# Layer ends of a float32 hybrid network: first tiles of the input before the weights, and all weight remainders on VectorE

## What is computed

```python
for layer in range(2):                      # attention, then the gated recurrence
    h = rmsnorm(x, pre_norm_w[layer])
    y = mixer(h, ...)                       # (o * silu(z)) @ w_out (+ b_out)
    x = x + rmsnorm(y, post_norm_w[layer])
h = rmsnorm(x, norm_w)                      # third layer: GLA and a delta rule side by side
merged = concat([gla_out, rwkv_out])
x = x + merged @ w_out
return rmsnorm(x, final_norm_w)
```

## Time and profile before

| | us |
|---|---|
| median of 3 runs | 3806.75 (3806.06 to 3808.11) |
| the profiled execution, its own time | 3811.12 |
| its span, from first to last instruction | 3809.8 |
| PE busy | 3559.3 (93%) |
| PEld busy | 2743.4 (72%) |
| DVE busy | 1993.4 (52%) |
| ACT busy | 1653.6 (43%) |
| POOL busy | 1196.5 (31%) |

### The profile page before, as it was taken

One profiled execution on the slowest core, in us unless ns is written; L12 is line 12 of the kernel. 1 busy time (PEld: TensorE's weight loads), 2 busy tenths in 40 slices (PEclk: granted clock), 3 DMA queues, 4 the chain that ended last, 5 costly groups with the idle time before them and its releaser, 6 DMA issues.

```text
span 3809.8 us, 80205 instructions
## 1 busy us (share of the span) xinstructions
PE 3559.3 (93%) x33632; PEld 2743.4 (72%) x33632; DVE 1993.4 (52%) x4558; ACT 1653.6 (43%) x3040; POOL 1196.5 (31%) x1470
## 2 busy tenths in 40 slices
PE   7899989999799999999997979999999997999799
PEld 4555557778678887878785867777777775788677
DVE  4655554255555556555553445656667665343322
ACT  2444443132455556555553334443444442444422
POOL 0000001132444445454544323222222220444432
PEclk9999999999899999999997989999999998999999
DMA  3000000132211010111111332111111113222322
GB/s 123 34 1 1 1 12 17 34 118 87 68 28 41 23 45 23 40 29 38 30 34 72 133 126 56 41 41 41 41 41 41 40 36 107 77 73 67 100 78 89
DMA packets 220230, 202.76 MB, mean 53 GB/s; under 512 B 7072, under 2 KB 191840, under 8 KB 219872
## 3 DMA queue, kind: packets, MB, share of 16 engines
q1 hardware_dynamic: 219872, 197.62, 16.8%
HBM read 164.04 MB, written 33.55 MB: 52 GB/s over the span
## 4 chain that ended last, share of the span: by engine, by line
PE 77%; DVE 9%; ACT 7%; POOL 3%; issue 3%; DMA 1%; SPq 0%; POOLq 0%; ACTq 0%; DVEq 0%
PE bank L194 18%; PE bank L196 16%; PE bank L195 16%; PE bank L452 5%; ACT arena L188 3%; PE bank L2386 2%; DVE arena L690 2%; PE bank L1236 2%; PE bank L2397 2%; ACT L282 1%; ACT arena L189 1%; PE bank L492 1%; PE bank L316 1%; PE bank L2400 1%; PE bank L2455 1%
## 5 line engine op out<-in xcount | busy, mean ns | idle before, releaser
L195 PE MATMUL bank<-hT_cut,arena_cut 128*128 128x512 f32 x2080 | 820.2, 394 | 0.0
L188 ACT ACTIVATE arena<-bank 128x512 f32<-128x512 f32 (+1 forms) x584 | 314.8, 569 | 559.4 <-PE bank L196 332.0
L194 PE MATMUL bank<-hT_cut,arena_cut 128*128 128x512 f32 x1112 | 501.2, 451 | 9.2 <-DVE arena L183 9.2
L188 ACT ACTIVATE arena<-arena 128x512 f32<-128x512 f32 (+3 forms) x690 | 353.6, 550 | 263.1 <-POOL arena L1426 192.0
L195 PEld LDWEIGHTS bank<-hT_cut,arena_cut 128*128 128x128 f32 x2080 | 394.9, 190 | 82.2 <-issue 18.5
L196 PE MATMUL bank<-hT_cut,arena_cut 128*128 128x512 f32 x1112 | 439.0, 395 | 0.0
L189 ACT ACTIVATE arena<-arena 128x256 f32<-128x256 f32 (+2 forms) x336 | 210.3, 627 | 503.2 <-DVE arena L178 276.9
L194 PE MATMUL bank<-arena_cut,hT_cut 128*128 128x512 f32 (+1 forms) x960 | 366.8, 382 | 56.4 <-POOL oT_cut L999 51.4
L195 PE MATMUL bank<-arena_cut,hT_cut 128*128 128x512 f32 (+1 forms) x960 | 360.0, 375 | 0.0
L2662 POOL TENSOR_TENSOR arena_cut<-arena,arena_cut 128x256 fp32r<-128x256 f32 x272 | 219.2, 836 | 433.0 <-ACT arena_cut L188 433.0
L194 PE MATMUL bank<-oT_cut,arena_cut 128*128 128x512 f32 x712 | 311.1, 437 | 29.9 <-DVE hT_cut L2708 16.4
(11 more groups left out here) (238 smaller groups left out, 7067.3 us busy)
## 6 DMA issues: line engine op xcount, KB each, us to landing
arena<-in_w_in SPq DMA_DIRECT2D x100, 512.0 KB, 3.9
arena<-in_rec_w_in SPq DMA_DIRECT2D x64, 512.0 KB, 4.1
x_after<-arena SPq DMA_DIRECT2D x32, 512.0 KB, 2.6
arena<-x_after SPq DMA_DIRECT2D x32, 512.0 KB, 4.1
oT<-in_x SPq DMA_DIRECT2D x16, 512.0 KB, 3.5
arena<-in_x SPq DMA_DIRECT2D x16, 512.0 KB, 3.5
h_after<-hT SPq DMA_DIRECT2D x4, 2048.0 KB, 7.7
hT<-h_after SPq DMA_DIRECT2D x4, 2048.0 KB, 16.8
```

The source lines that it names most:

```text
L188: return e.activation(out, a, f, bias=bias, scale=scale)
L194: pe.matmul(out, a[0], b[0], start=start, stop=False)
L195: pe.matmul(out, a[0], b[1], start=False, stop=False)
```

## The change

At all three layer ends:

- ScalarE first waits for the steps in the new list `k.ready` (one of TensorE and one of VectorE, named by each phase: what the memory of tiles 0 and 1 of oT and hT waits for), then does `cut(0)`, two early pieces, `cut(1)`, the other early pieces, and only then `settle` and the later pieces.
- GpSimd starts with the remainders of tiles 0 and 1, then `settle`. It subtracts no weights.
- VectorE subtracts all eight pieces, the early ones ahead of its `settle`, each in one instruction of 1024 columns.
- TensorE waits for one semaphore, `w_v`, piece by piece in the same order as before.

```diff
@@ attention_gate @@
     k.freed = [(0, z_pe.by("z", (KC - 1) * NG - 1))]
+    k.ready = [z_pe.by("z", (KC - 1) * NG), z_v.by("o", (KC - 1) * NG)]
...
@@ finish_layer @@
-    freed = dict(k.freed)
+    freed, ready = dict(k.freed), k.ready
...
-    w_a, w_v, w_p = k.steps("wo_rounded", "hi"), k.steps("wo_rest", "lo"), k.steps("wo_first_rest", "lo")
+    w_a, w_v = k.steps("wo_rounded", "hi"), k.steps("wo_rest", "lo")
...
-                    pe.wait_ge(*(w_p.by("lo", early.index(c)) if c in freed else w_v.by("lo", later.index(c))))
+                    pe.wait_ge(*w_v.by("lo", order.index(c)))
...
-        for c in early:
+        for done in ready:
+            a.wait_ge(*done)
+        cut(0)
+        for c in early[:2]:
+            rounded(c)
+        cut(1)
+        for c in early[2:]:
             rounded(c)
         k.settle(a)
-        cut(0)
-        cut(1)
         for c in later:
             rounded(c)
...
-        for n, c in enumerate(early):
-            pool.wait_ge(*w_a.by("hi", n))
-            for i in range(4):
-                part_of = slice(256 * i, 256 * i + 256)
-                ins = pool.tensor_tensor(wo_lo[:, c, part_of], wo[:, c, part_of], wo_hi[:, c, part_of], ALU.subtract)
-            ins.then_inc(*w_p.did("lo"))
-        k.settle(pool)
         cut(0)
         cut(1)
+        k.settle(pool)
...
-        k.settle(v)
-        for n, c in enumerate(later):
-            v.wait_ge(*w_a.by("hi", len(early) + n))
+        for n, c in enumerate(early + later):
+            if n == len(early):
+                k.settle(v)
+            v.wait_ge(*w_a.by("hi", n))
             v.tensor_tensor(wo_lo[:, c, :], wo[:, c, :], wo_hi[:, c, :], ALU.subtract).then_inc(*w_v.did("lo"))
...
@@ recurrence @@
+    k.ready = [Fpe.by("v", UN - 2), Bv.by("out", UN // 2 - 1)]
@@ gla @@
+    k.ready = [Fpe.by("z1", UN - 1), Bv.by("out1", 1)]
```

More of the change, by code:

```diff
@@ L204, in __init__ @@
         self.every, self.stores, self.known = [], [], {}
-        self.before, self.freed = [], []
+        self.before, self.freed, self.ready = [], [], []
         self.bank = [ctx.enter_context(nc.psum_tensor(f"bank{i}", [P, 512], F32))[:, :] for i in range(8)]
```

## The result

The changed kernel takes 3781.52 us in the median (3779.83 to 3782.65, 4 runs) against 3806.40 for the kernel before in the same comparison. The ratio is 0.9929, with a 95% interval of 0.9918 to 0.9941. It is faster by 24.9 us, clear of what a measurement can miss. Two repeats on later occasions gave 3779.25 against 3807.79 (ratio 0.9924, 0.9912 to 0.9936) and 3778.87 against 3806.23 (0.9926, 0.9913 to 0.9938), so the three differences are 24.9, 28.5 and 27.4 us. The profiled execution took 3782.65 us with a span of 3781.2, 28.6 less than the span before.

What follows compares the result with a forecast made beforehand. TensorE was taken as the bound, waiting 51.4 us for tile 0 on GpSimd at three layer ends. Gains of 0.8 + 11.2 + 11.9 = 23.9 us from 3806.75 gave a median of 3783 us, range 3773 to 3792.

Steps and rivals of the forecast that it cites:

- What bounds it: TensorE, 77% of the chain; its waits for tile 0's remainder on GpSimd, 51.4 us at three layer ends, are the target.
- 48th matmul: Last matmul of tile 0 at each layer end; its start measures the end, forecast gains 0.8, 11.2 and 11.9 us.
- The line of subtractions: At the long layer ends, eight VectorE pieces and four GpSimd tiles take turns: 19.1 us at most, taken as 18.8.
- The first end: First layer end: one early piece, transfers hold piece 2, TensorE runs through from 764.3; gain 0.8 us, sign uncertain.
- the rise at the old moment: First layer end: TensorE's clock rises when it did before, putting tile 0's last matmul at 775.2 instead of 776.0.
- The sum: Gains at the three layer ends, 0.8 + 11.2 + 11.9 = 23.9 us, under half of the 51.4 us of waits.
- rival 1: VectorE and GpSimd subtractions exclude each other less; tile 0's start sets its end: gain 34.5 us, 3772 us; chance 0.08.
- Rivals 2 and 3: TensorE's clock low through tile 0: 3798.5 us, chance 0.08; low on into tile 1: 3817 us, chance 0.04.
- Rival 4: Gain eaten later, or ScalarE reaches tile 0 later than the code order says: 3805 us; chance 0.06.
- The signs to look for: TensorE's waits ahead of tile 0 shrink from 51.4 to some 20 us, ended by L1063; restarts near 760.7, 2041.6, 3605.

Runs made afterwards that it cites:

- the two runs with tiles moved: Changed kernel, with GpSimd waiting for VectorE's eighth piece before tile 2 in one run, before tile 1 in the other: 3775.00 and 3774.16 us.
- the run with the order alone: Changed kernel's ScalarE order, but GpSimd still subtracts the early pieces as in the kernel before: 3797.08 us against 3805.47, ratio 0.9979.
- the kernel with tiles 1 to 3 later: Changed kernel, with GpSimd waiting for VectorE's eighth piece before tile 1: 3774.16 us; repeated, 3774.51 against 3778.87 for the changed kernel.

## Why the forecast was right, point by point

- **What bounds it, and that a gain at a layer end is kept.** Right: 176.3 us behind the last 48th matmul in both kernels.
- **The line of subtractions.** Forecast: 8 x 1.21 + 4 x 2.36 = 19.1 at most, taken as 18.8 us. Measured: 18.3 us at the second end. The 48th matmul was forecast at 58.1 - 37.5 = 20.6 us and, at the third end, 21.6 - 0.7 = 20.9 us after VectorE's last write began; it came at 19.9 and 20.2. Gains of 11.9 and 12.6 us instead of 11.2 and 11.9.
- **The first end.** The step that was mis-sized. Its own working gives 776.47 - 776.0 = 0.5 us or, with the rise at the old moment, 1.3, and 0.8 was put between them. Piece 2 was forecast 7.5 us after VectorE's last write and came at 7.35, but the forecast added 11 more matmuls at 0.43 from there. The clock rose at the second of them, and the gain was 2.5 us. In the thirteen profiles of this study the number of low pitches at this end was between 0 and 12 with no order that I can name, so that this term erred on the gainful side was luck.
- **The sum.** 27.0 us in the layer ends against a forecast of 23.9; the median moved by 24.9, and by 28.5 and 27.4 in the repeats. The range said to reach down to rival 1 stopped at 3773, 1 us above it.
- **Rival 1, no exclusion (3772 us).** Refuted by the durations, and by the two runs with tiles moved. The rule of the Trainium skill, page "SBUF — State Buffer", section "Who interferes with whom", agrees with the trace: 2.36 + 1.21 = 3.57 against 3.41 measured.
- **Rivals 2 and 3, the clock stays low.** They did not occur in the changed kernel, where the clock rose after 5 to 7 low pitches and stood at 1.00 in spite of the pause of 1.68 us (columns as in the earlier trace rows):

```profile
2035.00:2045.00 10.00, 5.90 (x15) 4.27 (x16) 9.59 (x6) 9.46 (x10) 5.71 (x2) 0.55 0.86 305
2045.00:2055.00 10.00, 8.32 (x36) 6.32 (x36) 8.23 (x5) 1.75 (x4) 6.80 (x2) 1.00 0.16 65
```

The mechanism is real, though, and the run with the order alone met a part of it, with pauses of 1.7 to 3.1 us: 14 and 18 low pitches, not the whole tile, and at its third end a fall from 1.00 back to 0.50. The Trainium skill (page "TensorE: Matmul & The Clock Gate", section "HAM oscillation — how this bites in real kernels") tells of a kernel that falls back in each wait of some 3 to 5 us. The trace agrees with it in kind at that third end. In the changed kernel the pauses are shorter, 0.34 and 1.68 us, and the one of 1.68, at the high level, cost no level.
- **Rival 4, the gain is eaten or does not come.** Refuted by the tail and by ScalarE's row at 2033.72.
- **The signs to look for.** TensorE's first matmul was forecast 3.9 to 4.3 us after the start of VectorE's last write and came at 4.13 to 4.20. The waits ahead of tile 0 were forecast at some 20 us and sum to 5.67 + 6.33 + 8.15 = 20.15, all ended by L1063. The pause of about 2 us between two pieces came too, as 1.68 at the second end and 1.66 at the third.
- **Where my understanding was short** is in the experiments. I expected 3788 us of the order alone and it took 3797: I summed the durations of GpSimd's pieces but did not follow TensorE through the pauses between them, nor its clock.

## What to carry to other kernels

When a wait ends with X, ask what would end it if X were instant: here the start of tile 0 moved by 14 to 16 us and its end by 12, since a line of subtractions on two engines that shut each other out took over as the limit. Count such instructions of both engines as one queue, and take out of it what nobody waits for yet; moving tiles 2 and 3 behind the weights was worth another 4.6 us in the layer ends. And of a change with two halves, try each alone: moving the work to the faster engine gave 24 of the 27 us, the new order 9 by itself.

## What the runs showed of the hardware that I had not expected

- In the run with the order alone TensorE worked in groups of six matmuls with pauses between them. At the second end (pauses of 2.71 and 3.10 us) its clock stayed at 0.50 for 14 pitches. At the third (1.73, 3.10 and 0.66 us) it stood at 1.00 from 3605.5 to 3608.8, mostly within the pause, and was at 0.50 again from 3609.0 to 3615.6 although TensorE was then busy for 5.94 of 6.60 us. In the changed kernel a pause of 1.68 us, behind some 30 matmuls without a gap at the high level, did not bring it down.
- The clock's rise does not follow the start of the work alone: with the same program and first matmuls 4.1 to 4.2 us after the same event, the two profiles of the kernel with tiles 1 to 3 later had 10, 9, 8 and 4, 11, 8 low pitches at the three ends.
- A remainder of 128x1024 takes VectorE 1.21 us and GpSimd 2.34 to 2.38. In a line that both share, moving one from GpSimd to VectorE shortens the line, though VectorE's own queue becomes longer (60.0 us in the layer ends with the weights on VectorE, 84.2 before).
